# Four reordered places on ScalarE and VectorE, and gates that sum both parts of h in the same columns

## The reference: what is computed

```python
for l in range(DEPTH):                      # 2
    h = rmsnorm(x, g[0])
    y = even_mixer(...) if l % 2 == 0 else odd_mixer(...)
    x = x + rmsnorm(y, g[1])
    h = rmsnorm(x, g[2])
    x = x + rmsnorm(sq_relu_mlp(h, mlp_w1[l], mlp_w2[l]), g[3])
# sq_relu_mlp(h, w1, w2) = square(relu(h @ w1)) @ w2, 4096 wide

# odd_mixer: two gates for each of 4 heads are the last 8 columns of h @ w_in
# hybrid_layer (last block): the gates are 8 columns of h @ w_in
h = rms_norm(x, g_pre) * (1 + scale) + shift
beta = sigmoid(beta_logit)
g = -exp(a_log) * softplus(a_logit + dt_bias)
o_dn = gated_delta_rule_chunked(l2_normalize(q_dn), l2_normalize(k_dn), v_dn, g, beta)
```

## Time and profile before

| | |
|---|---|
| median of 3 executions | 904.07 us (903.41 to 905.92) |
| the profiled execution, its own time | 905.36 us |
| its span, first to last instruction | 903.6 us |
| mean granted clock of TensorE | 0.997 of full |
| busy: TensorE, VectorE, ScalarE | 99%, 72%, 55% |
| instructions | 13,328 |

### The profile page before, as it was taken

One profiled execution on the slowest core, in us unless ns is written; L12 is line 12 of the kernel. 1 busy time (PEld: TensorE's weight loads), 2 busy tenths in 40 slices (PEclk: granted clock), 3 DMA queues, 4 the chain that ended last, 5 costly groups with the idle time before them and its releaser, 6 DMA issues.

```text
span 903.6 us, 13328 instructions
## 1 busy us (share of the span) xinstructions
PE 891.5 (99%) x5612; PEld 758.8 (84%) x5612; DVE 648.4 (72%) x787; ACT 497.3 (55%) x669; POOL 31.1 (3%) x25
## 2 busy tenths in 40 slices
PE   8999999999999999999999999999999999999997
PEld 6989888888888888798888888888778998888885
DVE  6898746569777777688466977777668795556655
ACT  7865456474444454755566544445557783256624
POOL 0000000000000000000000000000000083000000
PEclk9999999999999999999999999999999999999999
DMA  9634443365666663543346566666335343324331
GB/s 360 264 142 158 169 140 140 140 245 215 242 231 243 228 244 146 210 141 139 140 140 234 221 242 228 239 246 243 140 124 229 139 140 142 103 108 148 137 136 47
DMA packets 24155, 165.40 MB, mean 183 GB/s; under 512 B 2688, under 2 KB 2944, under 8 KB 4896
## 3 DMA queue, kind: packets, MB, share of 16 engines
q1 hardware_dynamic: 22608, 159.73, 48.2%
q0 software_dynamic: 1056, 4.34, 1.3%
q10 hardware_dynamic: 432, 0.49, 0.2%
HBM read 163.50 MB, written 1.05 MB: 182 GB/s over the span
## 4 chain that ended last, share of the span: by engine, by line
PE 92%; ACT 3%; DVE 3%; DMA 1%; issue 1%; DVEq 0%; ACTq 0%
PE acc L620 29%; PE lin L581 11%; PE lin L602 7%; PE lin L609 7%; PE lin L603 7%; PE lin L586 6%; PE lin L568 3%; PE lin L560 3%; PE lin L561 3%; PE acc L822 1%; ACT w_hi L1359 1%; DVE w_lo L1852 1%; PE acc L712 1%; PE acc L713 1%; PE acc L722 1%; PE lin L665 1%
## 5 line engine op out<-in xcount | busy, mean ns | idle before, releaser
L1852 DVE TENSOR_TENSOR w_lo<-raw,w_hi 128x2048 fp32r<-128x2048 f32 x137 | 318.7, 2337 | 134.6 <-ACT w_hi L1359 133.9
L1359 ACT CAST w_hi<-raw 128x2048 fp32r<-128x2048 f32 x137 | 260.1, 1906 | 148.6 <-DMA raw<-in_weights 97.0
L620 PE MATMUL acc<-w_hi,f_hi 128*128 128x512 f32 x288 | 113.3, 393 | 0.4 <-issue 0.4
L620 PE MATMUL acc<-w_hi,f_lo 128*128 128x512 f32 x288 | 112.4, 390 | 0.0
L602 PE MATMUL lin<-w_hi,h_both 128*128 128x512 f32 x272 | 110.1, 405 | 0.1
L603 PE MATMUL lin<-w_hi,h_both 128*128 128x512 f32 x272 | 107.2, 394 | 0.0
L581 PE MATMUL lin<-h_both,w_hi 128*128 128x512 f32 x448 | 106.7, 390 | 0.0
L581 PEld LDWEIGHTS lin<-h_both,w_hi 128*128 128x128 f32 x448 | 83.2, 188 | 16.7
L620 PE MATMUL acc<-w_lo,f_hi 128*128 128x512 f32 x288 | 79.1, 390 | 0.3 <-DVE w_lo L1852 0.3
L609 PE MATMUL lin<-w_lo,h_both 128*128 128x512 f32 x272 | 68.0, 390 | 0.2 <-DVE w_lo L1852 0.2
L560 PE MATMUL lin<-h_both,w_hi 128*128 128x256 f32 x272 | 67.2, 287 | 0.3 <-ACT arena L1575 0.3
(11 more groups left out here) (364 smaller groups left out, 1222.6 us busy)
## 6 DMA issues: line engine op xcount, KB each, us to landing
raw<-in_weights SPq DMA_DIRECT2D x149, 1024.0 KB, 4.8
rowbuf<-in_rows POOLq DMA_DIRECT2D x6, 512.0 KB, 4.0
x<-in_x_in SPq DMA_DIRECT2D x2, 512.0 KB, 4.6
raw<-in_weights SPq DMA_DIRECT2D x2, 512.0 KB, 7.2
arena<-in_const_even POOLq DMA_DIRECT2D x1, 1024.0 KB, 11.5
out<-x SPq DMA_DIRECT2D x3, 256.0 KB, 2.0
cst<-in_const SPq DMA_DIRECT2D x1, 580.0 KB, 8.4
out<-x ACTq DMA_DIRECT2D x1, 256.0 KB, 2.1
```

The lines of the kernel that those rows point to most:

```text
L620: return pe.matmul(acc[:, at:at + 512], part_of(2 * j + k)[i][:, t * P:(t + 1) * P], w[:, k * 1024 + c * 512:k * 1024 + (c + 1) * 512], st ...
L1359: act.copy(w_hi[:, o % SPLIT, :], raw[:, j % RAW, :]).then_inc(hi_done, 1)
L1852: dve.tensor_tensor(w_lo[:, j % RAW, :], r, hi.bitcast(F32), ALU.subtract).then_inc(tile_split, 1)
```

## The change

Five edits, in the order of the program:

1. MLP (both): ScalarE drops `ahead(up_0)` before `all_partitions_out`, so that this copy (the first tile of down_0) comes after the square instead. VectorE drops `ahead(up_0)` at the start, and calls it after the first `f_ready` instead; with it go three tiles, the second one of up_1 among them.
2. mq: ScalarE reads out the leading projection and the gate rows first, and then makes the copy of the second tile of mk.
3. Gates: hi and lo part of h go into the same 256 columns, as 16 products of 256 columns in place of 8 of 512. ScalarE copies 256 columns out, not 512, and turning needs two products, not four.
4. Last block, TensorE: `gates()` moves behind the whole of projection dz, and `gates_turned` into the first half of dq (after k=3 of its second half of columns); `decay_turned` moves from k=3 to the last k. `fill("dq", 0)` is the same work as `project_feature_major("dq", (0,))`.
5. Last block, ScalarE and VectorE: dz is read out before the copy of the second tile of dq and before the gate rows; Exp comes before Sigmoid; the remainder of the first tile of dv moves from before the series to after `rows_ready`, and that of the second tile from before the convolution of q to after it.

```diff
@@ TensorE
-            def project_feature_major(name, halves=(0, 1), between=None):
+            def project_feature_major(name, halves=(0, 1), between=None, behind=3):
-                            if between and b == 1 and k == 3:
+                            if between and b == 1 and k == behind:
                                 between()
@@ gates
-                    mm = pe.matmul(acc[0:16, 1536:2048], h_hi[:, 8, 16 * k:16 * (k + 1)], h_both[:, k, :, :].rearrange("p a t -> p (a t)"),
-                                   start=k == 0, stop=k == DC - 1)
+                    w = h_hi[:, 8, 16 * k:16 * (k + 1)]
+                    pe.matmul(acc[0:16, 1536:1536 + T], w, h_hi[:, k, :], start=k == 0, stop=False)
+                    mm = pe.matmul(acc[0:16, 1536:1536 + T], w, h_lo[:, k, :], start=False, stop=k == DC - 1)
@@ gates_turned
-                    pe.matmul(o, arena[0:16, CROSS + t * P:CROSS + (t + 1) * P], const_of("two", 16), start=True, stop=False)
-                    mm = pe.matmul(o, arena[0:8, CROSS + T + t * P:CROSS + T + (t + 1) * P], ident[0:8, 0:8], start=False, stop=True)
+                    mm = pe.matmul(o, arena[0:16, CROSS + t * P:CROSS + (t + 1) * P], const_of("two", 16), start=True, stop=True)
@@ last_lead
                 lead_turned_in_pair("dk")
+                project_token_major("dz", (1,), (1,))
                 gates()
-                project_token_major("dz", (1,), (1,))
-                gates_turned()
@@ the last block's start
             last_lead()
-            fill("dq", 0)
+            project_feature_major("dq", (0,), gates_turned)
             sum_squares("sqk")
-            project_feature_major("dq", (1,), decay_turned)
+            project_feature_major("dq", (1,), decay_turned, DC - 1)
@@ ScalarE, gate_rows_out
-                act.copy(arena[0:16, CROSS:CROSS + 512], acc[0:16, 1536:2048]).then_inc(gate_rows, 1)
+                act.copy(arena[0:16, CROSS:CROSS + T], acc[0:16, 1536:1536 + T]).then_inc(gate_rows, 1)
@@ ScalarE, mlp
                 lead_out(f"up{l}_0", 1, ACT.Relu)
-                ahead(f"up{l}_0")
                 all_partitions_out()
@@ ScalarE, mq
-            split_until(past("mq", 2))
             lead_out("mq", 0, ACT.Copy)
             lead_out("mq", 1, ACT.Copy)
             gate_rows_out()
+            split_until(past("mq", 2))
             ahead("mq")
@@ ScalarE, last block
             copy_out("dk", at("pre"), splits=False)
+            copy_out("dz", at("z"), ACT.Silu, False)
             split_until(LAST["dz"] + 2)
             gate_rows_out()
-            copy_out("dz", at("z"), ACT.Silu, False)
...
-            after(z_gate)
-            act.activation(by_tile(stat[:, 128:136]), by_tile(gate("z", 16))[:, :, 0:4], ACT.Sigmoid)
             act.activation(gate("ealog", 4), col("alog", 0, 4), ACT.Exp)
             after(abs_ready)
             act.activation(gate("e"), gate("mag"), ACT.Exp, scale=-1.0).then_inc(exp_ready, 1)
+            after(z_gate)
+            act.activation(by_tile(stat[:, 128:136]), by_tile(gate("z", 16))[:, :, 0:4], ACT.Sigmoid)
@@ VectorE, mlp
             def mlp(l):
-                ahead(f"up{l}_0")
...
                                       ALU.subtract).then_inc(f_ready, 1)
+                    if i == 0:
+                        ahead(name)
@@ VectorE, last block
             split_until(LAST["dz"] + 2)
-            split_until(LAST["dq"] + 1)
             rest_of_log1p()
...
             ins.then_inc(rows_ready, 1)
+            split_until(LAST["dq"] + 1)
+            conv("dq", S_AT["pre"] + 1024, S_AT["q"], "convd", 0)
             split_until(LAST["dq"] + 2)
-            conv("dq", S_AT["pre"] + 1024, S_AT["q"], "convd", 0)
             normalised("k", 1.0)
```

## The result

The changed kernel takes 912.84 us (median of 6 executions, 911.02 to 913.94). The kernel before took 905.30 us over 6 executions, the three shown above among them. The ratio is 1.0082, with a 95% interval of 1.0072 to 1.0092: slower by 7.5 us. The forecast was 911.0 us, in a range of 907.5 to 914.0; counted as a difference it was +6.97 us. The profiled execution of after took 911.15 us, with a span of 909.4.

What follows compares the result with a forecast made beforehand. The prediction took TensorE to bound the kernel, busy 891.5 of 903.6 us. Its terms, +6.54 (MLP starts), -0.42 (mq) and +0.85 (last block), sum to +6.97 on 904.07, giving 911.0 us, range 907.5 to 914.0.

Steps and rivals of the forecast that it cites:

- Bound by TensorE's stream: Whole kernel: TensorE is busy 891.5 of 903.6 us, so only its work or its stalls move the time.
- MLP starts, first wait: L586, both MLPs: up_1's second remainder is late, TensorE goes on at 206.80, and L620 starts 2.02 us later.
- MLP starts, second wait: L620's low products, both MLPs: TensorE waits 1.25 us more for the remainder of down_0's first tile.
- the clock's rival: MLP starts: clock falls in the new stalls, L586 at half pace, 0.6 to 1.7 us more per MLP; chance 0.15.
- mq: Behind mq: the 1.5 us wait for ScalarE goes, about 1.5 us comes at `gate_sums`; net -0.42 us.
- VectorE's delay: Behind mq: VectorE's pieces from the gate bias up to the end of the series come 0.73 us later.
- Gates: Each `gates()` on TensorE goes from 1.82 to 1.92 us, +0.10, counted within mq and the last block.
- The turning: Each `gates_turned` on TensorE goes from eight passes to four: -0.45 us, in mq and the last block.
- Last block: Two remainders ahead of VectorE's L2441 make it late for TensorE in `decay_rows`: +0.85 us net.
- VectorE starts its next piece at 698.15 in place of 698.25: Last block: the rows from L1009 come only 0.1 us earlier, so VectorE's following piece does too.
- The median: Whole kernel: the forecast's +6.97 us was added to a median of 904.07 us, giving 911.0 us.

Runs made afterwards that it cites:

- experiment 2: Kernel before, with only ScalarE's dropped `ahead(up_0)` at the MLP starts: 913.04 us, ratio 1.0091 to before.
- experiment 3: Kernel before, with only VectorE's `ahead(up_0)` moved behind the first `f_ready` at the MLP starts: 913.75 us, ratio 1.0095 to before.
- experiment 6: Changed kernel, with only up_1's second remainder put back ahead of f on VectorE: 906.56 us, ratio 1.0026 to before.
- experiment 7: Kernel before, with only ScalarE's new order behind mq: 905.26 us, ratio 0.9995 to before.
- experiment 8: Kernel before, with only the 256-column gates: 904.44 us, ratio 0.9988 to before.
- experiment 12: As experiment 11, but with `decay_turned` back at k=3 of dq's second half: 900.95 us, ratio 0.9953 to before.
- experiment 4: Kernel before, with ScalarE's `ahead(up_0)` dropped at the MLP starts and only down_0's first remainder behind f on VectorE: 904.15 us, ratio 0.9987.
- experiment 5: Changed kernel, with up_1's second remainder and ada0 back ahead of f on VectorE: 904.98 us, ratio 0.9998 to before.
- experiment 11: experiment 5 plus `gate_sums` later in mq and dv's second remainder behind the columns, `decay_turned` behind the last k: 901.94 us, ratio 0.9961 to before.

## Why the prediction was right, step by step

- **Bound by TensorE's stream.** Right: busy time grew by 1.0 us, the span by the stalls.
- **MLP starts, first wait.** Right in place and time: 206.75 for 206.80 in the first (0.05 us behind the remainder's end, for the 0.06 estimated), 2.2 us of idle time in both. Experiments 2 and 3 add what the forecast didn't say, that the two halves hold each other: ScalarE's alone costs 3.06 us per MLP by another way.
- **MLP starts, second wait.** Right in the second MLP (1.24 us, 1.25 forecast), and shown to be a due time of its own by experiment 6. That this MLP lost 3.47 us and not 3.27 comes half from L586, whose products took 2.01 us behind the wait and not 1.92, and half from behind the first low product (shift +4.90 to +5.01). In the first MLP the mechanism of the clock's rival came true, and not in the second: the low stretch cost 0.8 us in L586 (2.69 for 1.92) and 0.8 in the eight products behind it (2.70 for 1.92), and took the place of the second wait. The rival's price, 0.6 to 1.7 us more, was too high: this MLP lost 3.62 us and the other 3.47.
- **mq.** Right: -0.40 for -0.42, with the new wait at L1002. Edit 2 alone brought 0.16. Since VectorE ends last there, the 0.44 us that the turning saves on TensorE went into the wait (1.40 us in experiment 7, 1.63 in the whole change); that the other 0.24 come from ScalarE's copy of the gate rows (0.36 us for 256 columns, 0.56 for 512, ahead of the CAST for which VectorE waits) fits by size, and no run shows it alone. VectorE's delay was 0.64 us for the 0.73 forecast.
- **Gates.** The term of +0.10 each was mis-sized: -0.03 measured (experiment 8). I took 0.12 us per product from L586, but a product with 16 columns of weights runs at 0.114 (kernel after, in mq: 381.67 - 379.85 = 1.82 for 16). The Trainium skill, TensorE: Matmul & The Clock Gate, section Back-to-back issue gap, gave nearly equal times for both forms, and here the trace agrees with it. The size of one product by that rule, an estimate of 0.109 us, is below the 0.114 measured, and the measurement decides. The turning was right (-0.44 for -0.45).
- **Last block.** Right in sum (+0.66 for +0.85) and in cause, the second remainder ahead of the columns. One step failed: "VectorE starts its next piece at 698.15 in place of 698.25", because L1009 comes only 0.1 us earlier. Against the stream (a shift of 5.08), L1008 was 0.44 us earlier (700.56 for 695.92), since TensorE came to dq's second half 0.8 us ahead and not 0.6, and the wait that went was 0.56 us with its start-up. VectorE's next piece was 0.27 us earlier (703.06 for 698.25), and it was not L1008 that let the scan go but ScalarE's square root, for which VectorE waited until 701.09, behind the CAST and its table load. The series was ready 1.46 us earlier against the stream (L2403 at 699.32, its like at 695.70 before), and most of this was lost at the root, which the forecast did not have. Experiment 12 shows it: L1008 stands before the last four k, 1.0 us earlier against the stream, VectorE's scan starts at the same time within 0.02 us, and the wait ahead of L785 stays. So rows earlier than these would have gained nothing, and my number for this piece came near by luck. Which part of the earlier series comes from Exp ahead of Sigmoid and which from the remainder taken out, no run shows.
- **The median.** The forecast added its 6.97 to the median of three executions, 904.07; over six the kernel before is at 905.30, which is 1.2 of the 1.8 us by which the forecast was low. The terms come to 7.35 and not 6.97, and the clock moves both medians besides, so that 7.5 lies so near to 7.0 is in part luck.

## What to carry to other kernels

Give each piece of a helper engine the time at which the bound engine wants it, and when one piece is pulled forward, write down for each piece that it passes how much time is left until it is wanted: here f was worth 0.4 us, and it passed a remainder that was then ready 2.3 us after TensorE wanted it. In this kernel only the piece with the latest due time could be put behind, and then the gain was real (experiments 4 to 6). A removed wait is won only if the next engine in the chain is earlier too; behind mq the wait moved from ScalarE's read-out to VectorE's series, and 1.2 us were won only when TensorE's consumer was moved behind 12 other products. Single profiles of this kernel differ by 1.5 us per low stretch of the clock, so small edits are to be read from shifts at marked instructions and from medians of many runs.

## What the runs showed of the hardware

- The granted clock fell to 0.50 for 3.4 us behind the stall of the first MLP in each of the three profiles that have one (the changed kernel and experiments 3 and 2, idle 2.25, 2.40 and 3.25 us), and behind the like stall of the second MLP (2.22, 2.37 and 3.25 us) in none of them. So the length of the stall alone does not decide it. Where a wait followed, most of the cost was hidden (the first MLP lost 0.15 us more than the second in the changed kernel, 0.18 in experiment 3), where none did, it was 1.5 us.
- The low stretch at 413 of the kernel before was missing in the profiles of the changed kernel and of experiments 6, 7 and 11, and stood elsewhere in others, as in that of experiment 8 (stretch of that kernel):

```profile
381.80:385.20 3.40, 3.40 (x19) 3.40 (x19) 2.90 (x5) 2.32 (x5) 0.00 (x0) 0.55 0.35 147
```

  It moves a single profile by 1.5 to 1.6 us. What sets its place, no run here tells.
- A product of 256 columns takes 0.114 us with 16 columns of weights (mq of the changed kernel and of experiment 8) and 0.12 with 128 (L586).
- ScalarE's table load of 1.28 us ahead of one small square root, behind a CAST of 1.9 us, held VectorE for 1.5 us in the last block (experiment 12 and the changed kernel).
